# Two Fourier stages: folded tokens and folded input weights, and the sums of the output weights on GpSimd

## What is computed

```python
def fourier_mix(u):
    B, S, _ = u.shape
    ug = u.astype(jnp.float32).reshape(B, S, F_GROUPS, F_GROUP_DIM)
    y = jnp.fft.fft2(ug, axes=(1, 3), norm='ortho').real
    return y.reshape(B, S, F_WIDTH).astype(u.dtype)
...
def token_mix(h, w_in, w_fourier, w_ret, w_out):
    proj = h @ w_in
    offsets = np.cumsum(IN_SIZES)[:-1].tolist()
    u_f, q, k, v, g, a_f, a_r = jnp.split(proj, offsets, axis=-1)
    y_f = fourier_mix(u_f) @ w_fourier
    y_r = retention_branch(q, k, v, g) @ w_ret
    merged = jax.nn.sigmoid(a_f) * y_f + jax.nn.sigmoid(a_r) * y_r
    return merged @ w_out
```

## Time and profile before

| what | us |
|---|---|
| median of 3 runs (2945.31 to 2947.09) | 2947.02 |
| the profiled execution | 2945.48 |
| its span, first to last instruction | 2943.6 |
| PE busy | 2927.3 |
| GpSimd (POOL) busy | 1559.3 |
| DVE busy | 1533.1 |
| ACT busy | 1105.5 |
| mean of one ACT rounding of a unit, L1750 | 1.049 |
| mean of one ACT copy of a 512-column tile, L1758 | 0.599 |
| PE busy in the Fourier stage of layer 0, 111.22 us | 111.05 |

### The profile page before, as it was taken

How to read it: one execution, slowest core, us unless ns; L and a number is a source line. 1 busy time by engine, 2 the same in 40 slices (tenths; PEclk the granted TensorE clock), 3 DMA queues, 4 the chain that set the end, 5 groups by cost and what they waited for, 6 DMA issues and landing times.

```text
span 2943.6 us, 49397 instructions
## 1 busy us (share of the span) xinstructions
PE 2927.3 (99%) x19714; PEld 2451.0 (83%) x19714; DVE 1533.1 (52%) x2181; ACT 1105.5 (38%) x1663; POOL 1559.3 (53%) x1910
## 2 busy tenths in 40 slices
PE   9999999999999999999999999999999999999998
PEld 7877777788888888988888898888988888888887
DVE  5467787424556666753334274435542432473635
ACT  4454434333443332443433243323433342342323
POOL 6432233356546676546444556565465445575654
PEclk9999999999999999999999999999999999999999
DMA  5211111233326777423222223232233222223232
GB/s 172 92 45 41 42 54 57 93 143 101 122 97 221 253 273 252 148 79 128 85 92 72 93 87 115 86 107 85 94 108 115 78 77 94 93 94 99 95 100 72
DMA packets 92005, 320.50 MB, mean 109 GB/s; under 512 B 10112, under 2 KB 14336, under 8 KB 91520
## 3 DMA queue, kind: packets, MB, share of 16 engines
q1 hardware_dynamic: 84256, 301.34, 30.8%
q10 hardware_dynamic: 7520, 15.99, 1.6%
HBM read 313.36 MB, written 3.93 MB: 108 GB/s over the span
## 4 chain that ended last, share of the span: by engine, by line
PE 97%; issue 1%; POOL 1%; DMA 0%; DVE 0%; ACT 0%; SPq 0%; POOLq 0%; ACTq 0%; DVEq 0%
PE bank L826 26%; PE bank L830 25%; PE bank L827 25%; PE bank L1152 2%; PE bank L819 2%; PE bank L1163 2%; PE bank L820 2%; PE bank L821 2%; PE bank L1171 1%; POOL w_lo L757 1%; PE bank L858 1%; PE bank L857 1%; PE bank L856 1%; PE bank L1678 1%; PE bank L1677 1%
## 5 line engine op out<-in xcount | busy, mean ns | idle before, releaser
L757 POOL TENSOR_TENSOR w_lo<-w_raw,w_hi 128x256 fp32r<-128x256 f32 x1800 | 1464.8, 847 | 1044.5 <-ACT w_hi L1750 1034.5
L826 PE MATMUL bank<-act,w_hi 128*128 128x512 f32 (+1 forms) x3592 | 1363.0, 379 | 2.1 <-POOL w_lo L757 1.5
L830 PE MATMUL bank<-act,w_lo 128*128 128x512 f32 (+1 forms) x3592 | 1342.0, 374 | 0.0
L827 PE MATMUL bank<-act,w_hi 128*128 128x512 f32 (+1 forms) x3592 | 1340.9, 373 | 0.0
L826 PEld LDWEIGHTS bank<-act,w_hi 128*128 128x128 f32 x3592 | 676.7, 188 | 128.1 <-issue 9.3
L830 PEld LDWEIGHTS bank<-act,w_lo 128*128 128x128 f32 x3592 | 676.4, 188 | 120.5
L827 PEld LDWEIGHTS bank<-act,w_hi 128*128 128x128 f32 x3592 | 677.1, 189 | 111.0
L1750 ACT CAST w_hi<-w_raw 128x1024 fp32r<-128x1024 f32 x452 | 471.3, 1049 | 340.5 <-DMA w_raw<-in_weights 160.7
L1758 ACT ACTIVATE arena<-bank 128x512 f32<-128x512 f32 (+1 forms) x177 | 104.4, 594 | 416.5 <-PE bank L830 399.9
L775 POOL TENSOR_TENSOR stats<-stats,exponent 128x8 f32<-128x8 f32 (+2 forms) x38 | 46.6, 1226 | 299.5 <-DVE stats L2742 150.0
L2428 DVE TENSOR_TENSOR act<-tmp,act 128x512 fp32r<-128x512 f32 (+1 forms) x140 | 122.1, 872 | 77.6 <-ACT act L1777 72.7
(11 more groups left out here) (327 smaller groups left out, 2814.0 us busy)
## 6 DMA issues: line engine op xcount, KB each, us to landing
w_raw<-in_weights SPq DMA_DIRECT2D x469, 512.0 KB, 3.4
arena<-in_ada SPq DMA_DIRECT2D x96, 512.0 KB, 4.8
arena<-in_strips ACTq DMA_DIRECT2D x8, 448.0 KB, 3.6
arena<-in_x ACTq DMA_DIRECT2D x1, 2048.0 KB, 10.4
y_scratch<-tmp ACTq DMA_DIRECT2D x7, 256.0 KB, 2.0
arena<-y_scratch ACTq DMA_DIRECT2D x1, 1792.0 KB, 7.9
arena<-in_x SPq DMA_DIRECT2D x3, 512.0 KB, 7.8
arena<-in_lora_w ACTq DMA_DIRECT2D x8, 128.0 KB, 2.2
```

The lines of the kernel that those rows point to most:

```text
L757: ins = nc.gpsimd.tensor_tensor(w_lo[:, k, cols], weights_of(u)[:, cols], w_hi[:, k, cols].bitcast(F32), ALU.subtract)
L826: nc.tensor.matmul(o, wh, xh, start=first, stop=False)
L827: nc.tensor.matmul(o, wh, xl, start=False, stop=False)
L830: mm = nc.tensor.matmul(o, wl, xh, start=False, stop=last)
```

## The change

The input product is taken on folded operands. Where u is the normalised input, the cosine part of the spectrum needs only the sum of token s and token 512 - s, the sine part only their difference; and in the same way over features only sums and differences of the weights' columns. So:
- VectorE makes, in the second half of `split_halves`, sums and differences of each block of the first half (now kept in `FIRST_HALF`, in SBUF) with the mirrored block of the second (`fold`, four instructions), ScalarE rounds the folded block (`folded_high`) and VectorE makes its low part (`folded_low`). They lie in activation buffer A2.
- The weights come from a rearranged array, `w_in_four`: for each pair of groups an even and an odd unit, made by VectorE as sum and difference of two loaded units (`input_sums`, 1024 columns each), and one unit for the middle features. The eight input tiles of 512 columns give way to nine folded tiles (`folded_tile`): middle and even ones of 258 columns, odd ones of 256.
- Features and tokens are then multiplied for each pair of groups (`fourier_features`, `fourier_tokens`), the tokens with cosines of 257 columns and sines of 255.
- The gates come first: the layer's opening works on gates 0 to 2, then 3 and 4; the others are spread (`FOURIER_ORDER`). Each gate is kept in `MERGED` and not in a buffer of two.
- The sums of the output weights are made on GpSimd (`output_sums`), those of unit u + 1 ahead of the low part of u.

```diff
+FOURIER_ORDER = [("gate", j) for j in range(5)] + [("middle",), ("even", 0), ("odd", 0), ("even", 1), ("odd", 1), ("gate", 5),
+                                                   ("even", 2), ("odd", 2), ("even", 3), ("odd", 3), ("gate", 6), "out"]
+FOURIER_ORDER += [("out", j) for j in range(4)] + [("gate", 7)] + [("out", j) for j in range(4, 8)]
...
+        for what in FOURIER_ORDER:
+            if what == "out":
+                self.stages[f"fourier_in{l}"] = (start, len(self.tiles))
+                start = len(self.tiles)
+            elif what[0] == "gate":
+                gate(what[1])
+            elif what[0] == "middle":
+                add(folded, "middle", "w_in_four", KT * P, "A2")
+            elif what[0] in ("even", "odd"):
+                add(folded, what, "w_in_four", P * (2 * what[1] + (what[0] == "odd")), "A2")
+            else:
+                add(outs, what[1], "w_fourier_2", P * what[1], "A2", interleaved)
+        self.stages[f"fourier_out{l}"] = (start, len(self.tiles))
+        self.gates[f"fourier_out{l}"] = [gates[j] for j in range(KT)], [outs[j] for j in range(KT)]
...
-        p.plain(f"fourier_in{l}", "w_in_2", l, 0, 8)
-        p.split(f"fourier{l}", "A2", 8, before)
-        p.gated(f"fourier_out{l}", ("w_in_2", l, 5120, "A1"), ("w_fourier_2", l, 0, "A2"), 8, parts=True)
+        p.fourier(l)
...
+        def raw_free(eng, u):
+            if u in SUM_UNITS:
+                eng.wait_ge(sem("w_summed"), SUM_UNITS.index(u) + 1)
+            else:
+                low_made(eng, u)
...
+            for l in range(LAYERS):
+                if 0 <= q - splits[f"n1_{l}"][0] < KT:
+                    return FIRST_HALF[:, q - splits[f"n1_{l}"][0], :]
...
+            def output_sums(u):
+                i = SUM_UNITS.index(u)
+                pool.wait_ge(sem(f"w_landed{u % RAWS}"), 16 * (u // RAWS + 1))
+                low_made(pool, SUM_UNITS[i - 2])
+                raw, h = w_raw[:, u % RAWS, :], UNIT // 2
+                nc.gpsimd.tensor_tensor(W_SUMS[:, i % 2, 0:h], raw[:, 0:h], raw[:, h:UNIT], ALU.add)
+                nc.gpsimd.tensor_tensor(W_SUMS[:, i % 2, h:UNIT], raw[:, 0:h], raw[:, h:UNIT],
+                                        ALU.subtract).then_inc(sem("w_summed"), 1)
...
+                    if u + 1 in OUTPUT_UNITS:
+                        output_sums(u + 1)
...
+                cols = slice(S // 2, S) if what[0] == "odd" else slice(0, EVEN)
...
+                    nc.tensor.matmul(o, wh, xh, start=i == 0, stop=False)
+                    nc.tensor.matmul(o, wh, xl, start=False, stop=False)
+                    mm = nc.tensor.matmul(o, wl, xh, start=False, stop=i == KT - 1)
...
+                    for o, rows in ((banks[4][:, 0:WAVES], slice(0, P)), (banks[4][:, WAVES:2 * WAVES], slice(P, 2 * P)),
+                                    (banks[4][0:1, 2 * WAVES:3 * WAVES], slice(2 * P, 2 * P + 1))):
+                        nc.tensor.matmul(o, x[:, rows], COS_FEATURE, start=True, stop=False)
+                        nc.tensor.matmul(o, X_MIDDLE[0:KT, rows], MIDDLE_FEATURE[p], start=False, stop=True)
+                    for b in range(2):
+                        mm = nc.tensor.matmul(banks[5][:, P * b:P * (b + 1)], y[:, P * b:P * (b + 1)], SIN_FEATURE, start=True,
+                                              stop=True)
...
+                    nc.tensor.matmul(o, first, COS_TOKEN[0], start=True, stop=False)
+                    nc.tensor.matmul(o, second, COS_TOKEN[1], start=False, stop=False)
+                    return nc.tensor.matmul(o, last, LAST_TOKEN, start=False, stop=True)
...
+                for j in (3, 4):
+                    gate_tile(f"fourier_out{l}", f"n1_{l}", j)
+                folded_tile(l, "middle")
+                folded_tile(l, ("even", 0))
+                folded_tile(l, ("odd", 0))
+                folded_tile(l, ("even", 1))
+                fourier_features(0)
+                folded_tile(l, ("odd", 1))
+                gate_tile(f"fourier_out{l}", f"n1_{l}", 5)
+                fourier_features(1)
+                fourier_tokens(0)
+                folded_tile(l, ("even", 2))
+                folded_tile(l, ("odd", 2))
+                fourier_tokens(1)
+                folded_tile(l, ("even", 3))
+                fourier_features(2)
+                folded_tile(l, ("odd", 3))
                 fourier_tokens(2)
-                fourier_group(KT - 1)
-                gate_tile(f"fourier_out{l}", f"n1_{l}", 0, range(KT // 2 + 1, KT))
+                gate_tile(f"fourier_out{l}", f"n1_{l}", 6, range(KT // 2))
+                fourier_features(3)
+                gate_tile(f"fourier_out{l}", f"n1_{l}", 6, range(KT // 2, KT))
                 fourier_tokens(3)
                 fourier_nyquist()
-                gate_tile(f"fourier_out{l}", f"n1_{l}", 1)
...
+                def folded_high(i):
+                    if i > KT:
+                        j = i - KT - 1
+                        act.wait_ge(sem("nf_ready"), KT * l + j + 1)
+                        nc.scalar.copy(acts["A2"][:, 0, j, :], tmp[:, j % 2, :]).then_inc(sem("nf_high"), 1)
...
+                do(V_.tensor_scalar(TWICE, shifts_of(l, 0), 2.0, None, ALU.mult))
+                def fold(i):
+                    if i < KT:
+                        return
+                    dve.wait_ge(sem("high_done"), splits[f"n1_{l}"][0] + i + 1)
+                    j, shift = i - KT, shifts_of(l, 0)[:, i - KT:i - KT + 1]
+                    x, y, o = FIRST_HALF[:, j, :], normalised_half(splits[f"n1_{l}"][0] + i), tmp[:, j % 2, :]
+                    mirrored = y[:, W2 - 1:0:-1]
+                    do(V_.scalar_tensor_tensor(o[:, 1:W2], x[:, 1:W2], TWICE[:, j:j + 1], mirrored, ALU.add, ALU.add))
+                    do(V_.tensor_tensor(o[:, HALF_WAVES:S], x[:, 1:W2], mirrored, ALU.subtract))
+                    do(V_.tensor_scalar(o[:, 0:1], x[:, 0:1], shift, None, ALU.add))
+                    do(V_.tensor_scalar(o[:, W2:HALF_WAVES], y[:, 0:1], shift, None, ALU.add), "nf_ready")
+                def folded_low(j):
+                    dve.wait_ge(sem("nf_high"), KT * l + j + 1)
+                    do(V_.tensor_tensor(acts["A2"][:, 1, j, :], tmp[:, j % 2, :], acts["A2"][:, 0, j, :].bitcast(F32),
+                                        ALU.subtract), "nf_low")
+                def input_sums(p):
+                    i = (KT + KT // 2) * l + p
+                    u = SUM_UNITS[i]
+                    for v in (u, u + 1):
+                        dve.wait_ge(sem(f"w_landed{v % RAWS}"), 16 * (v // RAWS + 1))
+                    sums_free(i)
+                    x, y = w_raw[:, u % RAWS, :], w_raw[:, (u + 1) % RAWS, :]
+                    do(V_.tensor_tensor(W_SUMS[:, i % 2, :], x, y, ALU.add))
+                    do(V_.tensor_tensor(y, x, y, ALU.subtract), "w_summed")
+                def behind(i):
+                    if i > KT + 1:
+                        folded_low(i - KT - 2)
+                    if i == KT + 3:
+                        input_sums(0)
...
+                do(V_.memset(XS[:, :, 0:1], 0.0))
+                fold(2 * KT - 1)
+                folded_low(KT - 2)
+                folded_low(KT - 1)
...
-                def weight_sums(j):
-                    i = KT * l + j
-                    u = FOURIER_UNITS[i]
-                    dve.wait_ge(sem(f"w_landed{u % RAWS}"), 16 * (u // RAWS + 1))
-                    if i >= 2:
-                        low_made(dve, FOURIER_UNITS[i - 2])
-                    raw, h = w_raw[:, u % RAWS, :], UNIT // 2
-                    do(V_.tensor_tensor(W_SUMS[:, i % 2, 0:h], raw[:, 0:h], raw[:, h:UNIT], ALU.add))
-                    do(V_.tensor_tensor(W_SUMS[:, i % 2, h:UNIT], raw[:, 0:h], raw[:, h:UNIT], ALU.subtract), "w_summed")
...
+                do(V_.memset(NYQUIST.bitcast(F32), 0.0), "f_zeroed")
+                do(V_.memset(UF[:, :, 0:1], 0.0))
+                do(V_.memset(UF[:, :, S // 2:HALF_WAVES], 0.0))
+                input_sums(1)
+                residual(0)
+                residual(1)
+                input_sums(2)
+                rows = slice(64, 96)
+                dve.wait_ge(sem("f_rows_rounded"), l + 1)
...
-                    do(V_.tensor_tensor(dst, dst, g, ALU.mult), "gate_used")
-                    for i in range(j + 2, KT) if j == KT - 4 else range(j + 2, min(j + 3, KT - 2)):
-                        weight_sums(i)
+                    do(V_.tensor_tensor(dst, dst, JOINED, ALU.mult), "f_joined")
```

## The result

| | median us | range, runs | against before, 95% interval |
|---|---|---|---|
| before | 2947.06 | 2945.31 to 2947.33, 4 | |
| changed | 2975.66 | 2973.56 to 2978.42, 4 | 1.0099 [1.0081, 1.0116] |

A forecast was written before the change was run, and what follows sets the result against it. TensorE, busy 2927.3 of 2943.6 us, was taken to bound the kernel, by its own work or its waits. -32.0 + 30.3 + 9.8 = +8.1 us gave a forecast of 2955 us, range 2942 to 2971.

The forecast's parts named there:

- part 1: TensorE's own work in the Fourier stage after the opening: narrower folded products save 32.0 us over both layers.
- Part 2: Fourier opening: folds, folded low parts and first input sums in VectorE's queue make TensorE lose 30.3 us (26.7 to 35.9).
- Part 3: Behind the opening: TensorE waits 4.9 us per layer, 9.8 in all, mostly for GpSimd's low parts at the outputs.
- after it GpSimd catches up: Retention tiles behind the outputs: they take 5.45 us a unit, so GpSimd catches up; no cost put there.
- The two small waits ahead of the outputs: Ahead of the outputs, per layer: 0.9 us for even 1's low part and 0.1 before the second features.
- Rival 1: TensorE's clock falls in the opening: 1.1 to 6.5 us a layer, 3.8 in the middle; 2961.5 us; chance 0.22.
- The gate tile at half speed: Behind the opening: half clock costs up to one gate tile (5.45 us), within rival 1's price.
- Rival 2: Fourier stage: VectorE slows GpSimd throughout, wait before the outputs 12.8 instead of 4.9 us per layer; 2971 us; chance 0.15.
- Rival 3: No loss: the tokens' 257-column products cost 0.25 us like 128-column ones; 2946 us, down to 2937; chance 0.18.

The follow-up runs named there:

- The first try at this: The changed kernel with VectorE's folds moved behind the opening's last low part and gate 5 ahead of the middle tile: 2974.3 us, 1.0093.
- the ring opened: The changed kernel with output sums on VectorE and ScalarE copying each odd half before rounding the third output ahead: 2968.8 us, 1.0076.

## Why the prediction was wrong

The sign and the mechanism were right: part 1 gives, the opening eats it, the later waits decide. The sum, +8.1, was 24.6 short of the 32.7 measured (20.5 short of the medians' 28.6), and the time lies outside the range. By its own terms: -32.0 was -20.8, +30.3 was +36.1, +9.8 was +11.9, and +5.5 came behind the two stages, where nothing was put. The largest miss is TensorE's own work, and in it the price of the features:

- **Part 1, TensorE's work: 32.0 saved, measured 20.8.** Most of it is the features: 0.23 a product, measured 0.33. I priced all eight from products with 128 rows, and took the eight-row ones, three of eight, as no dearer. They and the products beside them take 0.31 to 0.42: 0.8 us a pair, 6.6 in all. Zero rows gave 4.4 of it back in the medians, 5.3 in the trace. The tokens, whose price no row showed, were close: 11.2 instead of 10.1 per layer. Gates and folded tiles took 27.6 and 26.6 us a layer where 27.2 and 25.9 were put, 2.2 in all, for which there is no run.
- **Part 2, the opening: 30.3, measured 36.1.** Right in kind: VectorE's queue sets the pace, and each instruction in it is paid in full. The first sums moved out gave 4.6 in the openings (5.0 expected), and with all the folds out the opening was back at 17.1 us, against 16.1 before. VectorE's own time, from the first normalisation to the last low part, grew by 17.2 us in each layer (in layer 0 from 8.90 to 26.08) where 16.4 was put; the fold at 1.47 instead of 1.37 is 1.4 of these 1.6. The half clock is 3.3, by the estimate above. The last 0.9 lies ahead of the second half's first normalisation.
- **Part 3, the outputs: 3.9 of wait per layer, measured 5.4 and 6.0.** The unit's price was nearly right (5.6 us, measured 5.7 to 5.9), and GpSimd's lead was even larger (14.9 us and not 12.3). But it stood 6.1 us for ScalarE's roundings (2.07 and 4.04 in layer 0) where 3.0 was put, which takes the longer lead back. Of its "after it GpSimd catches up" the opposite is true: it still lags at the value tiles, 2.4 and 2.3. Cutting the sums returned 13.9 in all. This is where the step failed in kind and not in size only: I ended the walk at the last output. The two small waits ahead of the outputs, 2.0 in both layers, were 0.5.
- **Rival 1, the clock**, did happen, near the lower end of its price: 1.7 and 1.6 us a layer, where 1.1 to 6.5 was put and 3.8 taken. It fell to 0.50 in the opening at about 1250.7, behind bursts of 1.2 us with pauses of 1.2 between them. The last two blocks ran without a pause (1267.05 to 1271.06) but still at half, and these are what it cost. It was back for the very first gate: 48 products of 512 columns took 10.98 us (1271.48 to 1282.46). The gate tile at half speed that I had priced in did not occur. The Trainium skill (TensorE: Matmul & The Clock Gate, "HAM oscillation — how this bites in real kernels") warns of bursts with pauses; the trace agrees on the fall, and the cost here was the 1.7 and 1.6 us.
- **Rival 2, GpSimd as the bound**, is half true, as above. **Rival 3** is false: the 257-column products with 128 rows start 0.43 us apart, the ones around the one-row product 0.53 and 0.63.

The prediction put GpSimd's 3.31 us for a gate's low part down to VectorE's sums of raw weights. In the kernel before with these sums on GpSimd it takes 3.29 still, beside a join's last multiplication.

That the change could pay at all rests on a placement that the prediction took as given. Folding needs some 20 us of VectorE per layer (eight times 2.2, and the first input sums), and three gates hide most of it, if ScalarE's copies, the raw weights and the input sums keep up. The first try at this showed the opening cured and the time unchanged; only the trace told that one from a dead end.

## What to carry to other kernels

When an engine gets more work per item, walk its queue to the first stretch where it truly stands idle, not to the end of the stage that changed: the lag here crossed into the next stage. When work moves off a critical queue, write down the same moment for each engine that must touch it (here ScalarE's copies and roundings), or it comes back as another wait. And judge an engine's load at an operation by what stands around it: GpSimd's sums were free where each output had a gate beside it and cost 14 us where eight outputs had one among them. And when a filler is put into a pause to hold up the clock, see what it itself delays before the saving is called the clock's price.

## What the runs showed of the hardware

- A full-precision product with an 8-row operand, between 128-row ones, is dearer than with 128 rows: 0.31 to 0.42 us against 0.22 for the same 130 columns. Filling the rows with zeros made the kernel 4.4 us faster. The one-row product of the tokens shows the same: it and the one before it take 0.63 and 0.53 us, the 128-row ones beside them 0.43. Why is open; whether the switch of rows or the few rows as such is meant, no run tells.
- The clock fell behind a stretch in which TensorE worked 4.0 of 7.4 us (1243.3 to 1250.7, a burst every 2.5), and stayed at half to 1271.06, through the 4 us of products without a pause at the end. Behind them it was at full speed again. In the output stage it dipped too, to 0.66 in the mean (1366 to 1371), behind one pause of 2 us.
- VectorE with two SBUF inputs and GpSimd slow each other by half and by a quarter (690 to 1030 ns, 778 to 983). The Trainium skill (SBUF — State Buffer, "Who interferes with whom") has them exclude each other; both being longer agrees with that. It takes back much of what moving work from one to the other gives: of the 14 us that GpSimd's sums cost, moving them to VectorE returned 2.6, and 6.9 with the ring opened.
- A one-column instruction on VectorE takes 0.21 us, half of a 255-column one (0.42).
